# Split weights kept in DRAM and loaded back as two parts in a one-core encoder layer

## The reference, cut to what matters

```python
h = _rmsnorm(x, g_pre_mix) * (1 + sc1) + sh1
proj = h @ w_in                                   # 1024 -> 2176
ya = pooling(proj)                                # three head groups on the columns of proj
yb = conformer_conv(proj)                         # causal depthwise conv of width 31, LayerNorm, swish
yc = short_conv(proj)
mix = concat(ya, yb, yc) @ w_out                  # 1024 -> 1024
x = x + gt1 * _rmsnorm(mix, g_post_mix)
h = _rmsnorm(x, g_pre_ffn) * (1 + sc2) + sh2
f = (silu(h @ w_gate) * (h @ w_up)) @ w_down      # 1024 -> 2816 -> 1024
x = x + gt2 * _rmsnorm(f, g_post_ffn)
```

## Time and profile before

| | |
|---|---|
| median of 3 runs | 2260.72 us (2260.14 to 2261.42) |
| span of the profiled execution | 2256.9 us |
| PE busy | 2241.4 us, 99% of the span |
| DVE busy | 1348.1 us, 60% |
| ACT busy | 1003.7 us, 44% |
| DMA queue of SP | 367.06 MB, packets on 47.8% of the time of 16 engines |
| read from and written to DRAM | 348.02 MB, 19.00 MB |

### The profile page before, as it was taken

How to read it: one execution, slowest core, us unless ns; L and a number is a source line. 1 busy time by engine, 2 the same in 40 slices (tenths; PEclk the granted TensorE clock), 3 DMA queues, 4 the chain that set the end, 5 groups by cost and what they waited for, 6 DMA issues and landing times.

```text
span 2256.9 us, 29984 instructions
## 1 busy us (share of the span) xinstructions
PE 2241.4 (99%) x12270; PEld 2069.5 (92%) x12270; DVE 1348.1 (60%) x1967; ACT 1003.7 (44%) x1419; POOL 38.2 (2%) x83
## 2 busy tenths in 40 slices
PE   9999999999999999999999999999999999999998
PEld 6779998979999988999898899989899998899987
DVE  3779966698444677744467854357784535443343
ACT  3455465454354534344544435254443425432332
POOL 0000000000000000000000000000000000000000
PEclk9999999999999999999999999999999999999999
DMA  9864654554443533544353363435335444444332
GB/s 375 310 218 168 239 202 140 177 169 166 170 151 129 181 127 122 186 150 154 126 185 123 123 213 122 157 123 187 122 127 181 123 131 154 154 150 159 123 129 94
DMA packets 103046, 368.98 MB, mean 163 GB/s; under 512 B 12631, under 2 KB 14807, under 8 KB 102396
## 3 DMA queue, kind: packets, MB, share of 16 engines
q1 hardware_dynamic: 102910, 367.06, 47.8%
HBM read 348.02 MB, written 19.00 MB: 163 GB/s over the span
## 4 chain that ended last, share of the span: by engine, by line
PE 89%; DVE 4%; DMA 1%; ACT 1%; issue 0%; SPq 0%; DVEq 0%; ACTq 0%
PE ps L650 89%; DVE wlo L1377 2%; DVE pr L1528 1%; DMA raw<-in_w_mix 1%; PE ps L720 1%; DVE early L1528 1%; PE ps L680 0%; DVE g_lo L1429 0%; ACT whi L980 0%; DVE h_lo L1422 0%; DMA raw<-in_w_gu 0%; ACT h_f L1048 0%; DVE xt L1446 0%; ACT junk L1003 0%; DVE pr L1550 0%
## 5 line engine op out<-in xcount | busy, mean ns | idle before, releaser
L1377 DVE TENSOR_TENSOR wlo<-raw,whi 128x1024 fp32r<-128x1024 f32 x531 | 646.6, 1222 | 521.9 <-ACT whi L980 520.6
L650 PE MATMUL ps<-h_hi,whi 128*128 128x384 f32 (+1 forms) x2808 | 920.9, 328 | 1.8 <-DVE h_lo L1422 1.0
L980 ACT ACTIVATE whi<-raw 128x1024 fp32r<-128x1024 f32 x531 | 560.8, 1058 | 811.6 <-DMA raw<-in_w_gu 528.7
L650 PE MATMUL ps<-h_hi,wlo 128*128 128x384 f32 (+1 forms) x2808 | 919.3, 327 | 0.0
L650 PE MATMUL ps<-h_lo,whi 128*128 128x384 f32 (+1 forms) x2808 | 919.2, 327 | 0.0
L650 PEld LDWEIGHTS ps<-h_hi,whi 128*128 128x128 f32 x2808 | 528.4, 188 | 7.0 <-issue 4.7
L650 PEld LDWEIGHTS ps<-h_lo,whi 128*128 128x128 f32 x2808 | 528.4, 188 | 0.5
L650 PEld LDWEIGHTS ps<-h_hi,wlo 128*128 128x128 f32 x2808 | 528.4, 188 | 0.0
L650 PE MATMUL ps<-whi,g_hi 128*128 128x512 f32 x748 | 235.1, 395 | 1.7 <-issue 0.9
L650 PE MATMUL ps<-whi,g_lo 128*128 128x512 f32 x748 | 231.1, 390 | 0.0
L650 PE MATMUL ps<-wlo,g_hi 128*128 128x512 f32 x748 | 230.8, 390 | 0.0
(11 more groups left out here) (148 smaller groups left out, 1313.6 us busy)
## 6 DMA issues: line engine op xcount, KB each, us to landing
raw<-in_w_gu SPq DMA_DIRECT2D x264, 512.0 KB, 3.3
raw<-in_w_mix SPq DMA_DIRECT2D x150, 512.0 KB, 3.3
raw<-in_w_dn SPq DMA_DIRECT2D x132, 512.0 KB, 3.3
xr<-in_x_all SPq DMA_DIRECT2D x29, 512.0 KB, 5.9
xr<-x_all SPq DMA_DIRECT2D x17, 512.0 KB, 5.8
pre<-in_w_ada SPq DMA_DIRECT2D x16, 512.0 KB, 10.4
x_all<-xr SPq DMA_DIRECT2D x5, 1536.0 KB, 7.5
xr<-in_w_ada SPq DMA_DIRECT2D x12, 512.0 KB, 7.9
```

Of the source, the lines that this page charges most:

```text
L650: return nc.tensor.matmul(out, lhsT, rhs, start=start, stop=stop, skip_group_check=True)
L980: nc.scalar.activation(whi[:, s, :], raw[:, s, :], ACT.Copy).then_inc(w_hi, 1)
L1377: tt(wlo[:, s, :], raw[:, s, :], whi[:, s, :].bitcast(F32), ALU.subtract).then_inc(w_lo, 1)
```

## The change

Of three of the four matrices the two parts of each unit are written to DRAM (`halves`, 47 units x 2 parts x 512 KB) the first time that a block splits them, and every later block loads the two parts straight into `whi` and `wlo` and splits nothing. For "in" the parts that are kept are those of block 1, for "out" and "dn" those of block 0. Gate and up are left as they were. All the new DMAs are SP's. The stores of unit n stand behind the load of unit n + 3 (`STORE_LAG`). SP waits for DVE's low part ahead of them. Before it loads over a slot whose parts are being stored it waits for the end of the stores, and before the first units that come from `halves` it waits for all the stores.

```diff
+SPLIT_IN = {"in": 1, "out": 0, "dn": 0}
+HALVES = NIN + NMIX + NF
+STORE_LAG = 3
+def kept(n):
+    return STREAM[n][0] in SPLIT_IN and STREAM[n][1] == SPLIT_IN[STREAM[n][0]]
+def from_halves(n):
+    return STREAM[n][0] in SPLIT_IN and STREAM[n][1] > SPLIT_IN[STREAM[n][0]]
+def split_here(n):
+    return not whole(n) and not from_halves(n)
...
         def landed(n):
-            return 16 * (n // RING + 1)
+            return sum(32 if from_halves(i) else 16 for i in range(n % RING, n + 1, RING))
...
-                sp.dma_start(raw[:, n % RING, :], source(n)).then_inc(w_landed[n % RING], 16)
+                if n >= RING and kept(n - RING):
+                    sp.wait_ge(halves_stored[n % RING], stored_halves(n - RING))
+                if from_halves(n):
+                    i = half_row(n)
+                    if i == 0 and STREAM[n][1] == 2:
+                        wait_halves(n)
+                    elif i in (NIN, NIN + NMIX) and STREAM[n][1] == 1:
+                        wait_halves(n)
+                    sp.dma_start(whi[:, n % RING, :].bitcast(F32), halves[0, i]).then_inc(w_landed[n % RING], 16)
+                    sp.dma_start(wlo[:, n % RING, :].bitcast(F32), halves[1, i]).then_inc(w_landed[n % RING], 16)
+                else:
+                    sp.dma_start(raw[:, n % RING, :], source(n)).then_inc(w_landed[n % RING], 16)
+                if n >= STORE_LAG and kept(n - STORE_LAG):
+                    keep_halves(n - STORE_LAG)
+
+            def keep_halves(n):
+                sp.wait_ge(w_lo, splits(n))
+                sp.dma_start(halves[0, half_row(n)], whi[:, n % RING, :].bitcast(F32)).then_inc(halves_stored[n % RING], 16)
+                sp.dma_start(halves[1, half_row(n)], wlo[:, n % RING, :].bitcast(F32)).then_inc(halves_stored[n % RING], 16)
...
             def wait_split(n):
-                pe.wait_ge(w_lo, splits(n))
+                if from_halves(n):
+                    pe.wait_ge(w_landed[n % RING], landed(n))
+                else:
+                    pe.wait_ge(w_lo, splits(n))
...
             def ahead(*key):
                 n = UNIT[key] + LEAD
-                if n < TOTAL and not whole(n):
+                if n < TOTAL and split_here(n):
                     high(n)
```

More of the change, by code:

```diff
@@ L102, with half_row @@
 WARM = (10, 2, 1)
+SPLIT_IN = {"in": 1, "out": 0, "dn": 0}
+HALVES = NIN + NMIX + NF
+STORE_LAG = 3
 def whole(n):
     return n < PARTS0 or PARTS1 <= n < NIN
+def half_row(n):
+    kind, _, i = STREAM[n][:3]
+    return {"in": 0, "out": NIN, "dn": NIN + NMIX}[kind] + i
+def kept(n):
[4 more added lines that the diff above has]
+    return not whole(n) and not from_halves(n)
 def splits(n):
-    return sum(not whole(i) for i in range(n + 1))
+    return sum(split_here(i) for i in range(n + 1))
 UNIT = {key: n for n, key in enumerate(STREAM)}
@@ L229, in build @@
           st_pool, st_conv, st_sconv, y_all, o_pool_p, o_conv_p, o_sconv_p,
-          o_pool_s, o_conv_s, o_sconv_s, x1_all, gates):
+          o_pool_s, o_conv_s, o_sconv_s, x1_all, gates, halves):
     ctx = ExitStack()
@@ L313, in build @@
         w_landed = [sem(f"w_landed{i}") for i in range(RING)]
+        halves_stored = [sem(f"halves_stored{i}") for i in range(RING)]
         x_landed = sem("x_landed")
@@ L381, in landed, with stored_halves @@
         def landed(n):
-            return 16 * (n // RING + 1)
+            return sum(32 if from_halves(i) else 16 for i in range(n % RING, n + 1, RING))
+        def stored_halves(n):
+            return 32 * sum(kept(i) for i in range(n % RING, n + 1, RING))
         def four_place(f, i):
@@ L475, in load, with wait_halves @@
                     sp.wait_ge(pre_used, group_under(n))
-                sp.dma_start(raw[:, n % RING, :], source(n)).then_inc(w_landed[n % RING], 16)
+                if n >= RING and kept(n - RING):
[16 more added lines that the diff above has]
+                sp.dma_start(halves[1, half_row(n)], wlo[:, n % RING, :].bitcast(F32)).then_inc(halves_stored[n % RING], 16)
+            def wait_halves(n):
+                for s in range(RING):
+                    kept_ = sum(kept(i) for i in range(s, n - STORE_LAG, RING))
+                    if kept_:
+                        sp.wait_ge(halves_stored[s], 32 * kept_)
             def load_x(b):
@@ L1920 @@
     aps.append(nc.dram_tensor("gates", (2, ROWS, D), F32, kind="Internal").ap())
+    aps.append(nc.dram_tensor("halves", (2, HALVES, P, D), F32, kind="Internal").ap())
     build(nc, *aps)
```

## The result

The changed kernel takes 2299.29 us (median of 4 runs, 2298.27 to 2302.29), the kernel before beside it 2260.43 us (4 runs, 2259.26 to 2261.42). The ratio is 1.0178, with a 95% interval of 1.0165 to 1.019: 38.9 us slower. I had forecast 17 us slower, within 2262 to 2310 us. The sign and the two places were right, the size was less than half of what came.

The account below looks back on a forecast made before the run. PE was taken to set the time almost everywhere. Losses of 8.5 us (dn 0) and 8.8 us (in 1 and out 0) sum to 17.3 us: 2274.2 us of span, 2278 us with 3.8 us around it; range 2262 to 2310 us.

Parts of the forecast that it names:

- the removed splits: 218 splits fewer on ACT (231 us) and DVE (266 us), all said to lie behind 453 us: gain nothing.
- The doubled loads are hidden: Later blocks: two DMAs per unit, 2.8 us, against PE's 4.1 us, issued 20 us ahead: no cost.
- The rate of the mixed queue: Stores and loads mixed at 378 GB/s, 1.39 us per DMA; at 415 about +1 us, at 348 +35.
- How much of that the ring's lead absorbs: dn 0: queue falls behind 1.13 us per unit; after the lead's part, 91.7 against 83.2 us, loss 8.5 us.
- out 0 and in 1, 8.8 us forecast: 50 stores there: demand 136.2 us against 127.4 us of room, which includes 8.5 us of ring lead.
- The hole in front of the x1 store: 176 to 184 us: engines nearly idle while SP stands before the x1 store; some 8 us can't be used.
- The waits added to SP: dn 0: SP's two new waits matter less; 8.4 us needed against 12, about 5 against 9.
- Stores dearer than loads: Rival: each further 512 KB store takes 2.45 us, not 1.39; loss from 38 us up to 115 us; chance 0.12.
- Hidden: Rival: at 415 GB/s or above, or with SP's pauses filled, the lead absorbs both backlogs: 2261 us; chance 0.12.
- PE's clock falls: Rival: stalls in dn 0 drop PE to 1.2 GHz, 29 us on top, 2307 us; chance 0.05.
- Faster: Rival: PE's matmuls speed up when ACT and DVE split less; at 6 ns each 2252 us; chance 0.05.
- what I said would show it: DMA share near 1.0, dn 0 units 3.4 us apart, PE waiting for DVE's low part, no pause after gu 1 begins.

Follow-up runs that it names:

- loads_paced: loads_only plus a DVE wait on ACT's copies, so that its taps come one unit at a time: 2260.42 us, 0.9996 of the kernel before.
- loads_only: Changed kernel storing only one unit, with all later blocks loading its two parts (later outputs not the reference's): 2264.47 us, 1.0018 of the kernel before.
- experiment 4: SP and ACT timelines of the changed kernel in dn 0, plus two edits of it, lead3 (2289.44 us) and g_first (2300.5 us).
- lead3: Changed kernel with units split three ahead of PE instead of four: 2289.44 us, 1.0126 of the kernel before.
- high_stores_only: Changed kernel with every block splitting as before and only the high part of each kept unit stored, all SP waits kept: 2268.37 us, 1.0033 of the kernel before.
- one_block_later: Changed kernel with the halves kept one block later (in 2, out 1, dn 1): 2267.78 us, 1.0033 of the kernel before.
- g_first: Changed kernel with `g_hi` and `g_lo` made ahead of the split in the down units: 2300.5 us, 1.0174 of the kernel before.
- experiment 6: Timelines of POOL's addition beside DVE's taps in the changed kernel and the one before, plus the run loads_paced: 2260.42 us, 0.9996 of the kernel before.

## Why the prediction was right and wrong

**What bounds the kernel, and the removed splits: right.** PE sets the time, and 218 splits less gave nothing (loads_paced 0.9996). One reading was off without harm: not all of the removed splits lie behind 453 us. Those of out 1 and in 2, 25 units, lie between 349 and 453 us; PE gained nothing there either (gu 0 to in 2: 239.0 and 238.8 us).

**The doubled loads are hidden: right for the queue, and one thing missed.** At 800 us the share is 0.86, and PE does not wait for a transfer. But I asked only what cover the splits had, not what they covered: as pauses in DVE's program they let POOL in. I had put this term at nothing; it is 3.3 us (loads_only), and it goes with the pacing (4.0 us less).

**The rate of the mixed queue: wrong, on the safe side.** I took 378 GB/s and said that at 415 the loss would be about 1 us. dn 0 ran at 413 GB/s, close to the 415 of the earlier trace rows, and the loss there was 14.3 us. So the error in this term hid part of the error in the next one. In out 0 and in 1 the rate was 356 GB/s at a share of 0.96, so 378 was about right there.

**"How much of that the ring's lead absorbs": this is the step that failed.** In dn 0 I let the whole lead count: PE two units before dn 0 at the first DMA, and the last unit used two units late, which let it absorb some 16 us (a backlog of 22 x 1.13 = 24.9 us against a loss of 8.5). Measured, from unit 3 (484.07 us) to unit 21 (553.33 us) the units begin 3.85 us apart (three transfers at 413 GB/s are 3.81) and not 3.03. 22 x 0.82 is 18.0 us, the loss is 14.3, so the lead absorbed 3 to 4 us. In its place stands the slack to where an in-order engine first waits for the load with PE's next need behind it, 3.1 us by the rows of experiment 4. I had PE wait for the low part of the weight; it waits for the low part of the data, `g_lo`, which stands behind the split of a later unit. In in 1 I credited another 8.5 us of lead.

**out 0 and in 1, 8.8 us forecast, 21.8 measured.** 31.65 MB were moved in 89.0 us (356 GB/s x 89.0). At my 378 GB/s that is 83.7 us, so 5.3 us more are rate and holes. The rest, 83.7 - 67.2 = 16.5 us, compares with my 8.8 plus the 8.5 us of lead. That these were not there is read from this sum, from ACT's waits and from lead3, which gives 9.7 us in this stretch; no run shows the size by itself. Seen from PE, the 21.8 us are 14.6 us of pauses and 7.2 us by which its busy time grew (74.38 us where it was 67.20), where the clock was low. The slow matmuls were a term that I had put at nothing in this stretch. The hole in front of the x1 store was in my sum (some 8 us) and was found: closing it gave 6.5 us in this stretch.

**The waits added to SP: right.** SP waits 27.7 us for stores in 17 places, but with the same waits and half of the stored bytes (high_stores_only) 26 of 33 us are gone, and dn 1 of one_block_later, with the same waits and longer units, loses nothing.

**The rivals.** *Stores dearer than loads* is refuted: with two stores to each load the queue ran at 413 GB/s. *Hidden* is refuted for the stores. *PE's clock falls* is wrong for dn 0, where I had put it: at 68.47 of 81 us busy, with a stall of 0.4 to 1.0 us in each unit from unit 3 on, the clock stayed at 1.00. The Trainium skill's "TensorE: Matmul & The Clock Gate", section "HAM oscillation — how this bites in real kernels", which I weighed there, describes a kernel in which every wait for a transfer throttles PE again; with the waits of dn 0 this row does not show it. The rival's mechanism holds in in 1, where I had not looked: during the pause of 8.9 us the clock falls to 0.50 (1.2 GHz), and at that level PE gets through 14 matmuls in 4 us and not 24. It falls twice more in this stretch, behind pauses of 2.0 and 1.7 us (at 216.7 and 229.5 us). Over the stretch the mean is 0.90. How much of the 21.8 us is the clock's was not measured by itself. The 7.2 us of added busy time are the most that the slow matmuls took; part of them ran while data was late anyway. *Faster* is refuted: 233 matmuls in 40 us, as before.

**Of what I said would show it,** the shares, SP's waits, the bytes (114.3 MB more read, 49.3 MB more written) and the chain in dn 0, from `g_lo` over ACT to a load of `raw`, were there. The mean spacing was 3.7 us (81.0 / 22) and not 3.4. PE waited for `g_lo` and not for the low part of the weight. DVE and ACT were busy for 1098 and 791 us, some 20 us more than I had said, since overlapping records hide that much of the splits. PE does pause after 600 us, which I had named as a sign against the mechanism; the pauses are POOL's and not a transfer's.

## What to carry to other kernels

When traffic is added to a ring that runs ahead, count its lead up to the first in-order instruction that waits for the load and has the next unit's work behind it, not up to where the bounding engine uses the data; here that was 3 us and not 16. Compare bytes and compute time stage by stage: in dn 0, where a unit keeps PE for 3.0 us, the stores cost 14 us, and in dn 1, where it keeps PE for 4.2 us, nothing. Expect that a stage which is made shorter runs into the next engine: of the 6.5 us that closing the hole gave in in 1, 4.0 were lost in the next stretch, in PE's waits for DVE's `h_lo` and `y_pr` and at a low clock. When work off the critical path is removed, look for who ran in the pauses that it made.

## What the runs showed of the hardware

- 81 us of mixed traffic, two stores to one load, nearly all of 512 KB, ran at 413 GB/s with a share of 1.02. The best 20 us of the kernel before, in which loads ran alone, reached 415, so the stores made no difference that these rows show.
- With the queue full, SP's own issue of a DMA grows from 0.33 us to between 1.17 and 1.52 us (the SP rows of experiment 4). In dn 1 of one_block_later, with the same three DMAs per unit and a share of 0.96 but no backlog, it is 0.33 to 0.63 us in all but one of its issues. Three such long issues take about as long as the unit's three transfers, so I read them as the queue's backlog pushing back; that was not tried by itself.
- The granted clock fell to about half (1.2 GHz) at pauses of PE of 1.7, 2.0 and 8.9 us in in 1, and of 2.3 us at gu 0 in two experiments. In dn 0, with 19 pauses of 0.4 to 1.0 us, and in g_first with one of 1.7 us among them, it stayed at 1.00. So the length of a pause alone does not tell.
- A short POOL instruction beside a train of DVE instructions waits for the train: 9.07 us and not 0.19 (experiment 6). The Trainium skill, page "SBUF — State Buffer", section "SBUF: two separate sides", says that DVE with two operands in SBUF and a GpSimd instruction that reads SBUF share a pair of ports under an exclusive lock, held for a whole instruction. The trace agrees that POOL is shut out, but it lasted for most of 21 instructions and not for one.
